# Index key columns computed feature-major in the gates' block, and turned by two transposes

## The reference, cut to what matters

```python
DSA_SPLITS = (DSA_Q_LATENT, DSA_KV_LATENT, IDX_DIM, IDX_HEADS)     # 128, 128, 32, 8
for l in range(DEPTH):                                            # 2
    h = rmsnorm(x, norm_mix_g[l])
    z = h @ w_in[l]                                               # 1024 x 6964
    z_dsa, z_rwkv, z_mlstm, z_fox, z_gate = _split(z, GROUP_SPLITS)
    y_dsa = dsa_mixer(*_split(z_dsa, DSA_SPLITS), ...)
    ...
def dsa_mixer(c_q, c_kv, k_idx, w_idx, ...):
    ki = rmsnorm(k_idx, g_kidx)
    wi = w_idx.astype(jnp.float32) * IDX_HEADS ** -0.5
    dots = jnp.einsum('bqhd,bsd->bqhs', qib, ki) * IDX_DIM ** -0.5
    score = jnp.einsum('bqh,bqhs->bqs', wib, jax.nn.relu(dots))   # then the 64 best keys of each query
def mlstm_mixer(q, k, v, o, i_pre, f_pre, ...):
    li = softcap(i_pre + b_i, GATE_SOFTCAP); lf = log_sigmoid(softcap(f_pre + b_f, GATE_SOFTCAP))
def fox_mixer(q, k, v, f_pre, b_f):
    lf = jax.nn.log_sigmoid((f_pre + b_f))
```

## Time and profile before

| what | value |
|---|---|
| time, median of three runs | 1676.49 us |
| span of the profiled execution | 1673.1 us |
| TensorE busy | 1614.6 us, 97% of the span |
| VectorE busy | 612.5 us, 37% |
| ScalarE busy | 446.8 us, 27% |
| layer 0, from the first product of `z_ml` | from 22.27 us |
| layer 1, the same | from 520.74 us |
| expert stretch with DMA at full share | about 850 to 1600 us |

### The profile page before, as it was taken

One profiled execution on the slowest core, in us unless ns is written; L12 is line 12 of the kernel. 1 busy time (PEld: TensorE's weight loads), 2 busy tenths in 40 slices (PEclk: granted clock), 3 DMA queues, 4 the chain that ended last, 5 costly groups with the idle time before them and its releaser, 6 DMA issues.

```text
span 1673.1 us, 34751 instructions
## 1 busy us (share of the span) xinstructions
PE 1614.6 (97%) x15676; PEld 1089.6 (65%) x15676; DVE 612.5 (37%) x1036; ACT 446.8 (27%) x693; POOL 32.3 (2%) x27
## 2 busy tenths in 40 slices
PE   6999999999999999999999999999999999899995
PEld 6987776899988987776866534565345643356431
DVE  3678775554644677766501010101101010010101
ACT  3564533453534554523201010000100010000101
POOL 0000030000000000030000000000000000000000
PEclk9999999999999999999999999999999999999998
DMA  6424312454654433413989999999999999999994
GB/s 254 177 101 149 140 60 106 153 201 165 243 197 142 162 124 132 146 52 134 429 307 353 383 429 428 424 427 425 428 427 425 424 427 427 427 426 424 426 429 168
DMA packets 41108, 472.75 MB, mean 283 GB/s; under 512 B 4544, under 2 KB 4544, under 8 KB 5632
## 3 DMA queue, kind: packets, MB, share of 16 engines
q1 hardware_dynamic: 40592, 468.86, 69.6%
q0 software_dynamic: 368, 1.65, 0.2%
HBM read 469.44 MB, written 1.05 MB: 281 GB/s over the span
## 4 chain that ended last, share of the span: by engine, by line
PE 85%; DMA 7%; DVE 4%; ACT 2%; issue 1%; SPq 0%; DVEq 0%; ACTq 0%
PE bank L608 72%; DMA pairs_high<-stream 4%; DMA pairs_low<-stream 2%; PE bank L1221 1%; PE bank L1285 1%; PE bank L690 1%; DVE ring_a_r L1708 1%; DVE arena L1708 1%; PE bank L984 1%; ACT high_a L1378 1%; DMA smalls<-small 1%; PE bank L895 1%; PE bank L976 1%; PE bank L804 0%; PE bank L1246 0%
## 5 line engine op out<-in xcount | busy, mean ns | idle before, releaser
L608 PE MATMUL bank<-pairs_high,hsel 128*32 128x256 f32 (+1 forms) x4320 | 334.6, 408 | 2.8 <-DMA pairs_high<-stream 2.8
L608 PEld LDWEIGHTS bank<-pairs_high,hsel 128*32 128x32 f32 (+1 forms) x4320 | 161.7, 113 | 159.9 <-issue 83.2
L1708 DVE TENSOR_TENSOR ring_a_r<-ring_a,high_a 128x2048 fp32r<-128x2048 f32 x82 | 188.0, 2297 | 125.7 <-ACT high_a L1378 125.6
L1708 DVE TENSOR_TENSOR arena<-arena,bank 128x256 f32<-128x256 f32 (+2 forms) x122 | 44.5, 392 | 464.2 <-ACT arena L1631 451.4
L1378 ACT ACTIVATE high_a<-ring_a 128x2048 fp32r<-128x2048 f32 x82 | 157.1, 1916 | 134.4 <-PE bank L608 117.1
L608 PE MATMUL bank<-pairs_high,actT 128*32 128x256 f32 (+1 forms) x2048 | 165.2, 413 | 7.7 <-DMA pairs_high<-stream 7.7
L608 PE MATMUL bank<-hT_h,ring_a_r 128*128 128x256 f32 (+1 forms) x592 | 167.4, 283 | 0.0
L608 PE MATMUL bank<-high_a,hT_h 128*128 128x512 f32 (+1 forms) x416 | 165.1, 397 | 0.8 <-issue 0.8
L608 PE MATMUL bank<-pairs_low,hsel 128*32 128x256 f32 (+1 forms) x1952 | 161.9, 415 | 0.2 <-DMA pairs_low<-stream 0.2
L608 PE MATMUL bank<-high_a,hT_l 128*128 128x512 f32 (+1 forms) x416 | 160.1, 385 | 0.0
L608 PE MATMUL bank<-ring_a_r,hT_h 128*128 128x512 f32 (+1 forms) x416 | 160.1, 385 | 0.0
(11 more groups left out here) (324 smaller groups left out, 1784.5 us busy)
## 6 DMA issues: line engine op xcount, KB each, us to landing
pairs_high<-stream SPq DMA_DIRECT2D x113, 2048.0 KB, 27.2
pairs_low<-stream SPq DMA_DIRECT2D x55, 2048.0 KB, 27.2
ring_a<-stream SPq DMA_DIRECT2D x107, 1024.0 KB, 4.8
consts<-const SPq DMA_DIRECT2D x1, 1079.0 KB, 7.1
resid<-x SPq DMA_DIRECT2D x1, 1024.0 KB, 4.9
y<-xn SPq DMA_DIRECT2D x2, 512.0 KB, 2.6
smalls<-small SPq DMA_DIRECT2D x1, 824.5 KB, 10.6
smalls<-small POOLq DMA_DIRECT2D x1, 824.5 KB, 7.0
```

Source lines behind the costliest of these rows:

```text
L608: ins = mm(o, lhsT, rhs, start=start, stop=stop)
L1708: return v.tensor_tensor(o, i0, i1, op)
```

## The change

The 40 index columns move into rows of the gates' block that carried nothing. The 8 head weights go to rows 4 to 11, the 32 keys to rows 96 to 127, and the block becomes 128 rows, all feature-major. The 24 matmuls of 40 columns in each half of `z_ml` are gone. DVE adds the bias to 128 rows in one instruction (the bias of the new rows is zero), and there is no copy of index columns there. A new step, `ds_idx`, stands behind `z_lat`: TensorE turns the two token tiles of `g_pre` with two transposes into bank 6, and DVE copies the 8 and the 32 columns to `z_idx`. `ds_norm` waits for that.

The words that name the change also speak of FoX and RWKV heads in turns on both row halves and of one mask product for several heads. Neither is in the diff: the head order `h = i % 2 + 2 * j` of `fx_L` and the mask product per head (`causal`) are the same in both kernels.

```diff
-    "z_ml": [..., (Z_FOX + 768, 4, 320), (256, 40, 352)],
+    "z_ml": [..., (Z_FOX + 768, 4, 320), (256, 32, 352), (288, 8, 260)],
-    "norm_mix", "z_ml", "z_lat", "z_mvo", "ds_norm", ...
+    "norm_mix", "z_ml", "z_lat", "ds_idx", "z_mvo", "ds_norm", ...
+        "ds_idx": [("dI", 6)],
...
             elif step == "z_ml" and side:
-                fm_part(bank(ep)[0:96, 0:T], n0, kk, 256, 96, last=False)
-                for tt in range(TT):
-                    ins = tm_part(bank(ep)[:, T + 40 * tt:T + 40 * tt + 40], n0, kk, tt, 352, 40, first=False, last=tt == 1)
+                ins = fm_part(bank(ep)[:, 0:T], n0, kk, 256, P)
...
+        def ds_idx(l):
+            drained(pe, l, "z_mlb")
+            begin(pe, l, "dI")
+            for tt in range(TT):
+                ins = nc.tensor.transpose(bank("dI")[:, tsl(tt)], g_pre[:, tsl(tt)], ident)
+            ins.then_inc(filled("dI"), 1)
...
             elif s == "z_ml":
                 full(ve, l, s + "b")
-                link(v.tensor_copy(z_idx, bank(s + "b")[:, T:T + 80].rearrange("p (a b) -> p a b", a=TT)))
-                ts(g_pre[0:96, :], bank(s + "b")[0:96, 0:T], s_(l, "gate_b")[0:96, :], ALU.add).then_inc(freed(s + "b"), 1)
+                ts(g_pre, bank(s + "b")[:, 0:T], s_(l, "gate_b"), ALU.add).then_inc(freed(s + "b"), 1)
+            elif s == "ds_idx":
+                full(ve, l, "dI")
+                turned_idx = bank2("dI", P)[:, 0:TT, :]
+                v.tensor_copy(z_idx[:, :, 32:40], turned_idx[:, :, 4:12])
+                v.tensor_copy(z_idx[:, :, 0:32], turned_idx[:, :, 96:128]).then_inc(freed("dI"), 1)
...
             elif s == "ds_norm":
                 drained(ve, l, "z_lata")
                 drained(ve, l, "z_latb")
+                drained(ve, l, "dI")
```

More of the change, by code:

```diff
@@ L42 @@
 GROUPS = {
-    "z_ml": [(Z_ML, 256, 0), (Z_ML + 768, 4, 256), (Z_ML + 772, 4, 288), (Z_FOX + 768, 4, 320), (256, 40, 352)],
+    "z_ml": [(Z_ML, 256, 0), (Z_ML + 768, 4, 256), (Z_ML + 772, 4, 288), (Z_FOX + 768, 4, 320), (256, 32, 352), (288, 8, 260)],
     "z_lat": [(0, 256, 0), (Z_FOX + 512, 256, 256)],
@@ L59 @@
 SCHEDULE = [
-    "norm_mix", "z_ml", "z_lat", "z_mvo", "ds_norm", "z_fox", "ds_tr", "ml_gate", "part:z_rw0", "part:z_rw0", "ds_q",
+    "norm_mix", "z_ml", "z_lat", "ds_idx", "z_mvo", "ds_norm", "z_fox", "ds_tr", "ml_gate", "part:z_rw0", "part:z_rw0", "ds_q",
     "z_rw0", "ds_dot0", "part:z_rw1", "ml_D", "ml_conv", "hi:gate00:0", "lo:gate00:0", "ml_in", "z_rw1", "ds_dot1", "part:gate00", "ml_qk", "part:gate00",
@@ L1096, in mixer @@
                     merged_transposes(l)
+                elif step == "ds_idx":
+                    ds_idx(l)
                 elif step == "ds_tr":
```

## The result

The changed kernel takes 1667.59 us (median of 5 executions, 1665.8 to 1671.25) against 1676.49 us of the kernel before (median of 5, 1675.8 to 1682.53): a ratio of 0.9938, with an interval of 0.9918 to 0.9957. The forecast was 1667.1 us. One execution each of three experiments took far longer than its others (2335, 3311 and 7345 us); medians are hardly moved by them, and they count nowhere else.

The account below looks back on a forecast made before the run. TensorE, busy without a gap, bounds the layers, and DMA the expert stretch. Each layer saves 4.94 - 0.25 = 4.7 us, both 9.4: 1673.1 to 1663.7, plus 3.4 gives 1667.1 us; range 1663.6 to 1673.0.

Parts of the forecast that it names:

- The index products: In z_ml, 128-row products replace gates and 40-column products: 2.54 us less a half, 5.08 us a layer.
- rival of nearly free products: In z_ml, 40-column products cost by their columns, 0.02 us each; time 1675.2 us; chance 0.05.
- The split chain: Ahead of z_lat, the weight piece's split on ACT and DVE becomes late; 0.1 to 0.2 us lost a layer.
- Transposes and DVE: Behind z_lat, two transposes cost 0.25 us a layer on TensorE; DVE's two short copies hide under 3.21 us idle.
- The gain lasts: Through both layers into the expert stretch, 4.7 us a layer stay, 9.4 in all; the expert stream starts earlier.
- swallowed gain: In the expert stretch, the stream's end does not depend on layer 1, hiding everything: 1676.5 us; chance 0.09.
- slower stream: In the expert stretch, the load rate falls 2.5% (421 to 410 GB/s), costing 17.8 us: 1684.9 us; chance 0.03.
- for what lies around it: Around the profiled span, 3.4 us added to 1663.7 us to reach the median, 1667.1 us.
- half as long again in both layers: From FoX's short logits products on, TensorE's half-clock time of 6.7 to 6.8 us lengthens, costing 3.4 us: 1670.5; chance 0.20.
- Half-clock stretches that differ by microseconds: In the layers' FoX logits stage, a changed length of TensorE's half-clock time would show the forecast wrong.

Follow-up runs that it names:

- the three series: The changed kernel, unaltered, measured three times against the kernel before: 1667.59, 1668.01 and 1667.29 us (the last as companion of the woven kernel).

## Why the prediction was right

**The index products.** Forecast were 2.54 us a half and 4.9 us a layer for `z_lat`; it came 4.84 us earlier in layer 0 and 4.85 in layer 1. The pace of 0.111 us by weight load held in both directions: put back, the products cost 0.103 each, and three times the columns cost hardly more (0.108). The Trainium skill's rule on loads ("TensorE: Matmul & The Clock Gate", section "LDWEIGHTS (loading the stationary operand)"), 107 ns, agrees. The rival of nearly free products falls.

**The split chain.** It became the path as reckoned, with a wait of 0.17 us for DVE's split ahead of layer 1's `z_lat` and 0.2 us of handover ahead of layer 0's second half. That second half began 4.60 us after the first where the text had 4.49: TensorE came 0.15 us after the split was ready (24.75 + 2.29 = 27.04 us), not 0.05.

**Transposes and DVE.** 0.22 us for 0.25, no wait for the bias addition; copies of 0.17 and 0.21 us under 3.26 us of idle time. Right in place and size; five times the transposes showed the price again. The 275 ns that the prediction set against its row are no other price: one transpose is in flight for 273 ns, and they overlap.

**The gain lasts.** 4.62 us a layer stood for 4.7, 9.25 for 9.4. The waits of SP's queue, 7.2 and 16.7 us, and the stream's rate did not move, and the first product of the experts came 2.5 us earlier (835.81 for 838.34 us), so an earlier layer 1 did start the stream's work earlier. The rivals of a swallowed gain and of a slower stream fall.

**Where the match is luck.** The median came within 0.5 us of the forecast; the medians of the three series lie 8.9, 9.2 and 13.0 us apart, so the last half microsecond is the draw of executions. And the 3.4 us added to the span "for what lies around it" were misread: each execution lists some 1.8 us between its span and its time (1669.5 and 1671.25 for the profiled one), and the rest is that the profiled execution of the kernel before was faster than its median. The forecast does not suffer, since it comes to the median less 9.4 us.

**Where the profile came out otherwise: the half-clock stretch.** Layer 1 was to start at about 516.0 us and started at 518.34, 2.3 us later: 0.3 because `z_ml` of layer 0 began later, 1.7 because layer 0's stretch was 10.2 us long, 0.1 because a layer gained 4.62 and not 4.7, and 0.2 that are left (a wait for a split in the dense stage grew from 0.9 to 1.3). This was a rival, "half as long again in both layers", 1670.5 us, and the profiled execution is that case (1671.25 us; that the two numbers are so near is luck too, since the routing stage and the 3.4 us above come into it). Half-clock stretches that differ by microseconds were also named as a sign of being wrong; the sign came, and it did not touch the gain. What the text had wrong is its kind: it was put as an effect of where the work lies, to be had or not. The repeats show that it changes from one execution of the changed kernel to the next, and the listed clocks that the mean clock does so in both kernels; so it widens the spread and hardly moves the difference. The text also left out the third place, the routing stage, which moves by as much.

**What the text did not see.** The removed products can bring the clock down themselves. The profile before has no half-clock stretch in `z_ml`, so none was priced. But in three other profiled kernels with these products (put back; the kernel before with a moved quarter, and woven) one of 3.4 us stands in layer 1's `z_ml`, 1.5 us of time each, and with twice as many they stand in both layers. That the kernel before has it in a part of its executions, and that this is why the medians lie 8.9, 9.2 and 13.0 us apart in the three series, is likely and not shown.

## What to carry to other kernels

Where every matmul has its own stationary operand, count matmuls, not columns, as far as this case shows it: 40, 128 and 256 moving columns cost 0.10 to 0.12 us each, but 512 cost 0.23 (48 in the 11.15 us of `z_lat`). Laying narrow columns feature-major into idle rows of a block that is loaded anyway then takes the whole price away, and turning the result by a transpose costs about one such matmul. Then follow the chain that fed the shortened stage; here it had 2.4 us to spare and became the path. And before reading a difference of a few microseconds from two profiles, compare the granted clock of the executions: it was halved here behind runs of narrow products, for a time that changes from one execution to the next, and weaving dense products in between, in small steps, brought a median 5.5 us lower in one series, and 1664.2 us in the next.

## What was not expected of the hardware

- TensorE, busy without a gap, is granted 0.50 of its clock behind a run of products of 40 columns (3.4 and 6.8 us long), and 1.00 behind the same number of products of 128 columns with the same weight loads. The 128-column ones are done 2.4 us sooner.
- The half-clock stretches measured about 3.4, 6.8 or 10.2 us, once 13.7 (routing stage, short products put back); in one program the same place had 10.2 and 6.8 us in different executions, and the routing stage 10.2, 6.8 and 3.4.
- The same moved quarter took the stretch away in one layer and not in the other; woven in steps of one weight block, dense products kept the clock in both, in the two profiled executions of the changed kernel; other executions list a lower mean clock, and where they lost it no profile shows. In those two the routing stage had no half-clock stretch either, although nothing was changed there. Why is open.
